# Retention scores of a fused two-block transformer: one f32 product per tile replaced by three products of rounded and remainder parts

## The chip, the cores and the metric

The kernel runs on one core of one Trainium2 chip. The metric is the device time of one launch in microseconds (us); where several runs are shown, the median is meant. The engines are TensorE (PE, with its weight loads listed as PEld), VectorE (DVE), ScalarE (ACT), GpSimd (POOL) and SyncE (SP), each with its own stream of instructions; they meet only in semaphores.

## The reference

Two blocks run one after the other on a sequence of 512 positions of width 1024; each has two layers. The change concerns the first block, whose layers begin with a projection of the normalised input and use its first 1024 columns as queries and keys of a retention with four heads of 128 channels:

```python
q = rotary(q.reshape(B, S, RET_HEADS, RET_QK_DIM), positions)
k = rotary(k.reshape(B, S, RET_HEADS, RET_QK_DIM), positions) * (RET_QK_DIM ** -0.5)
...
scores = jnp.einsum('bnihd,bnjhd->bnhij', qc, kc) * decay_intra.astype(dt)
intra = jnp.einsum('bnhij,bnjhe->bnihe', scores, vc)
...
o = rms_norm(o).reshape(B, S, RET_V_WIDTH)
return jax.nn.silu(g) * o
```

`rotary` multiplies the two halves of the 128 channels by cosines and sines of the position. The reference works in chunks of 128 with a carried state; the kernel computes the same sum directly over all causal pairs of positions, with the decay as a table. Everything is f32.

## The kernel before

**Layout and products.** All activations lie transposed, channels on the 128 partitions, positions along the free axis (S = 512). A wide product is made of three products of rounded operands: a value a is kept as aH (a rounded to the type fp32r) and aL = a - aH, and `three` (lines 575 to 579) sums wH·aH, wH·aL and wL·aH in PSUM. The weights come as a stream of 648 tiles of 128 x 1024, each good for 128 output columns (`tile_T`, 8 k-steps of three products, 24 in all) or, in `tiles_N`, for a quarter of 512 output columns whose results lie token by token.

**The ring.** Four slots hold the stream. SP loads tile n + 4 into `raw` when DVE has read tile n out of it (semaphore lo_ready, lines 401 to 404 and 427 to 432). ACT rounds it into `hi` (line 1316), as soon as it has landed and PE is done with the tile that used the slot (tile_done). DVE subtracts (line 1846: `lo` = raw - hi) and raises lo_ready, on which PE waits. Both engines do this in a function `tick` (ACT line 1306, DVE line 1835), which runs three tiles ahead of the tile at which it is called. Results go to PSUM banks 0 to 3 in turn; PE waits for bank_free before it uses a bank again.

**The stage of the change.** In each of the two layers the first eight tiles give the queries of heads 0 to 3 (n = 0 to 3) and the keys (n = 4 to 7). For tile n DVE runs `rotate(n)` (lines 2210 to 2221): two multiplications by cosine and sine tables and one on the other half of the channels, all from PSUM (lines 2215 to 2217, the last raises bank_free), a drain, an addition (line 2220) that leaves the rotated tile in A[:, n], a drain that raises rope_ready. The loop on DVE is `tick`, then `rotate` (lines 2223 to 2227); ACT only runs its ticks there (line 1527), and so has nothing to wait for but the slot. Tiles 0 to 2 of PE are computed together (`first_tiles`, `first_tiles_halved`), tile 3 alone, tiles 4 to 7 by `tiles_T`.

The next eight tiles are the values (`tiles_N(1)` twice, lines 642 to 658). Its first tile, tile 8 here, uses all four banks in turn, t = 0 to 3, with six products for each, and waits before each t for that bank, which `rotate(4 + t)` sets free.

**The scores.** `scores(h)` (lines 878 to 889) makes four products per head, one for each block j of 128 keys, of widths 512, 384, 256 and 128, from the f32 tiles A[:, 4 + h] and A[:, h]. DVE multiplies each by the decay (line 2233); the product j = 3 waits until DVE has read j = 0, because they share a bank. `scores(0)` comes after the first `tiles_N(1)`, `scores(1)` after the second, `scores(2)` and `scores(3)` between the products with the values (`weighted`, line 898) and the sums of squares (`square_sum`, line 908), which wait for ACT and POOL.

The order on each engine is written out by hand; there is no planner.

Of the kernel before, what the change touches and what calls it, by code (L numbers as in the profile page):

```python
# [7 lines left out]
F32 = mybir.dt.float32  # L8
F32R = mybir.dt.float32r
I32 = mybir.dt.int32  # L10
ACT = mybir.ActivationFunctionType
ALU = mybir.AluOpType
AX = mybir.AxisListType

P = 128
S = 512
# [4 lines left out]
R_HEADS, R_V = 4, 256  # L21
# [5 lines left out]
RING = 4  # L27
# [67 lines left out]
def build(nc, stream, first, xT, cvec, pos, consts, decay, tables, vec1, ws, bs, vec2, wf, outT):  # L95
    with ExitStack() as ctx:
# [3 lines left out]
        def sem(name):  # L100
            return ctx.enter_context(nc.semaphore(name))
# [19 lines left out]
        A, B, M = act3[:, 0:KT], act3[:, KT:2 * KT], act3[:, 2 * KT:3 * KT]  # L121
# [19 lines left out]
        pb = ctx.enter_context(nc.psum_tensor("pb", [P, 8, S], F32))  # L141
# [20 lines left out]
        rr_head = lambda h: yF[:, (6 + h % 2) * S:(7 + h % 2) * S]  # L162
        sqH = lambda h: yL[:, h % 2]
        sqL = lambda h: yL[:, 2 + h % 2]
        sumH, sumL, root_sq = halved[:, 4], halved[:, 5], act3[:, 7]
        meanF = meanR[:].bitcast(F32)
        root_y = yF[:, 14 * S:16 * S].rearrange("p (a s) -> p a s", a=2)
# [33 lines left out]
        score_bank = lambda h, j: (6, 7, 4 if h < 2 else 1, 6)[j]  # L201
# [76 lines left out]
        tile_done = sem("tile_done")  # L278
# [44 lines left out]
        x_added = sem("x_added")  # L323
        y_ready = sem("y_ready")
        rope_ready = sem("rope_ready")
        score_full = sem("score_full")
        score_ready = sem("score_ready")
        o_full = sem("o_full")
# [237 lines left out]
        def _(pe):  # L566
# [299 lines left out]
            for l in range(LAYERS):  # L866
# [10 lines left out]
                o_bank = lambda h: 2 + 2 * (h % 2)  # L877
                def scores(h):

                    pe.wait_ge(rope_ready, rope.value() + 5 + h)  # L880
                    for j in range(TT):
                        if j == 0 and h:

                            pe.wait_ge(score_ready, sc.value() + 4 * h)
                        if j == 3:

                            pe.wait_ge(score_ready, sc.value() + 4 * h + 1)
                        pe.matmul(pb[:, score_bank(h, j), 0:S - j * P], A[:, 4 + h, j * P:(j + 1) * P], A[:, h, j * P:S],
                                  start=True, stop=True).then_inc(score_full, 1)

                def weighted(h):

# [406 lines left out]
        def _(act):  # L1299
# [31 lines left out]
            def tiles_T(n, drain, uses_st=True, last=False, peel=False, ada=False, x_steps={}):  # L1331
                def body(i, first=False):
                    for s in range(RING):
                        t = None if not last else TILES - RING * (n // RING - i) + s
                        if ada:
                            for j in ADA_TICKS[s]:
                                tick(j, ada=j < RING)
                        elif s or not first:
                            tick(s, t)
                        act.wait_ge(tile_done, done.next())  # L1340
                        drain(i, s)
                if peel:
                    body(0, True)
                    bodies(n // RING - 1, {**({stf: RING} if uses_st else {}), **x_steps}, lambda i: body(i + 1))
                    return
                bodies(n // RING, {**({stf: RING} if uses_st else {}), **x_steps, **(dict(ada_ring) if ada else {})},
                       body, last)
# [166 lines left out]
            for l in range(LAYERS):  # L1514

                def drain_to(first, func):
                    def drain(i, s):
                        act.activation(act3[:, at(i * RING + s + first), :], pb[:, s:s + 1], func  # L1518
                                       ).then_inc(bank_free, 1)
                    return drain  # L1520

                def drain_tok(first, func):
                    def drain(i, t):
                        act.activation(act3[:, bass.ds(i + first + 2 * t, 1), :], pb[:, t:t + 1], func
                                       ).then_inc(bank_free, 1)
                    return drain
                tiles_T(8, lambda i, s: None, uses_st=False, peel=True)
                tiles_N(2, drain_tok(8, ACT.Copy))

                def head_out(h):  # L1530

                    for e in range(2):
                        o = pb[:, 2 + 2 * (h % 2) + e]
                        act.wait_ge(o_full, of.next())
                        act.activation(A[:, h + 4 * e], o, ACT.Copy)
                        act.activation(Osq[h % 2][:, e * S:(e + 1) * S], o, ACT.Square, scale=R_V ** -0.5
                                       ).then_inc(osq_ready, 1)

                def root_of(h):

                    act.wait_ge(summed, sums.next())
                    if h >= 2:
                        act.wait_ge(o_normed, 1 + 8 * l + 2 * (h - 1))
                    act.activation(r_head(h), pb[:, mean_bank(h)], ACT.Abs_reciprocal_sqrt, bias=epsc)
                    act.drain()
                    act.activation(rr_head(h), r_head(h), ACT.Square).then_inc(rooted, 1)

                def rounded_sum(h):

                    act.wait_ge(osq_added, oa.next())  # L1550
                    act.activation(sqH(h), Osq[h % 2][:, 0:S], ACT.Copy).then_inc(osq_rounded, 1)

                act.activation(cs[:, 2, 0:1], epsc, ACT.Abs_reciprocal_sqrt)
                head_out(0)
                rounded_sum(0)
                head_out(1)
                root_of(0)
                rounded_sum(1)
                head_out(2)
                root_of(1)  # L1560
                rounded_sum(2)
                head_out(3)
                root_of(2)
                rounded_sum(3)
                root_of(3)
                tiles_T(8, lambda i, s: to_st(s, func=ACT.Silu))
                pairs(True)
                tiles_N(2, drain_tok(8, ACT.Gelu_apprx_tanh), ada=True)
                act.wait_ge(v_mean, means.next())
                act.activation(stat[:, 8:12], stat[:, 12:16], ACT.Sqrt).then_inc(rooted, 1)  # L1570
                tiles_T(8, drain_to(0, ACT.Gelu_apprx_tanh), uses_st=False, ada=True)

                for n in range(KT):
                    s = n % RING
                    tick(s)
                    act.wait_ge(tile_done, done.next())
                    act.wait_ge(y_ready, l * 56 + (8 + n + 1))
                    act.activation(A[:, n], pb[:, s], ACT.Copy).then_inc(bank_free, 1)
                pairs()
                for g in range(4):  # L1580
                    tick(g)
                    act.wait_ge(tile_done, done.next())
                    for e in range(2):
                        n = 2 * g + e

                        to_st(n % 4, scale=v1[:, span(l * V_ALL + (V_PS + n), 1)], bias=bpps[:, n:n + 1])
                pairs(True)
                tick(0)
                to_x_halved(mod[:, 24:32], peel=True)
                tiles_T(8, lambda i, s: to_st(s), peel=True)  # L1590
                with repeat(act, 3, {split: 16, done: 16, stf: 8, **{c: 64 for c in land}}):
                    tiles_T(8, lambda i, s: None, uses_st=False)
                    tiles_T(8, lambda i, s: to_st(s))
                if l < LAYERS - 1:
                    to_x_halved(mod[:, 0:8])
                else:
                    act.wait_ge(gain_ready, 1)
                    late_tiles(to_late(hH, gain2, double=True))
# [213 lines left out]
        def _(dve):  # L1812
# [395 lines left out]
            for l in range(LAYERS):  # L2208

                def rotate(n):  # L2210

                    f = 1.0 if n < R_HEADS else float(P) ** -0.5
                    q = pb[:, n % RING]
                    dve.wait_ge(tile_done, done.next())
                    dve.scalar_tensor_tensor(A[:, n], q, f, cosT, ALU.mult, ALU.mult)
                    dve.scalar_tensor_tensor(rT[upper], q[lower], f, sinT[lower], ALU.mult, ALU.mult)
                    dve.scalar_tensor_tensor(rT[lower], q[upper], f, sinT[upper], ALU.mult, ALU.mult
                                             ).then_inc(bank_free, 1)
                    dve.drain()
                    dve.tensor_tensor(A[:, n], A[:, n], rT, ALU.add)  # L2220
                    dve.drain().then_inc(rope_ready, 1)

                for n in range(2 * R_HEADS):
                    if n:
                        tick(n % RING)
                    drained.next()
                    rotate(n)

                def decayed(h):
                    for j in range(TT):  # L2230
# [589 lines left out]
```

## Time and profile before

| | us |
|---|---|
| median of 3 runs | 3257.05 (3256.15 to 3257.8) |
| the profiled execution, its own time | 3255.68 |
| its span, first to last instruction | 3253.2 |
| PE busy | 3227.9 |
| DVE busy | 1900.5 |
| ACT busy | 1173.0 |
| POOL busy | 191.9 |

The span is the part of the execution that the trace covers; 2.5 us of the time lie around it. Busy time of PE counts from the start of a product to its modelled end, so neighbours overlap and gaps are hidden in it; the distance of two starts says more. In a timeline a row is start, duration, engine, line, operation, output <- input, count, and in brackets the idle time before it with the instruction that ended it.

### The profile page before, as it was taken

The page shows a single profiled execution, that of the slowest core. Times are in us where ns is not written, and L with a number is a line of the kernel's source. Part 1 is how long each engine was busy: PE and PEld are TensorE (multiplying, and loading weights), DVE is VectorE, ACT ScalarE, POOL GpSimd, SP SyncE. Part 2 cuts the span into 40 slices and gives each one's busy share as a digit, 9 for nine tenths or more (in the row PEclk, how much of TensorE's full clock was granted, in tenths as well). Part 3 has the DMA queues.
Part 4 walks back from the last instruction along what each step waited for, and adds up shares of the span by engine and source line. Part 5 has one row for each costly group of instructions (what it writes and reads, how often), then busy time and mean ns, then how long its engine had stood idle before and what let it go on. Part 6 is the DMA issues. An engine that isn't in the chain of part 4 may idle for free.

```text
span 3253.2 us, 43481 instructions
## 1 busy us (share of the span) xinstructions
PE 3227.9 (99%) x15288; PEld 2678.3 (82%) x15288; DVE 1900.5 (58%) x2749; ACT 1173.0 (36%) x1557; POOL 191.9 (6%) x202
## 2 busy tenths in 40 slices
PE   8999999999999999999999999999999999999998
PEld 7788888888888788888888888778888888988887
DVE  7454667564447454667564445656665744586656
ACT  4433333332223433343332233364333523453323
POOL 2100000100001100000100002021000101010001
PEclk9999999999999999999999999999999999999999
DMA  6146424422222145424422222202322322123222
GB/s 250 59 155 202 141 91 162 149 97 97 97 97 91 59 157 199 140 88 166 143 97 97 97 97 88 85 21 97 104 97 97 104 97 91 46 73 103 97 97 78
DMA packets 100057, 357.81 MB, mean 110 GB/s; under 512 B 11328, under 2 KB 13648, under 8 KB 99808
## 3 DMA queue, kind: packets, MB, share of 16 engines
q1 hardware_dynamic: 99248, 353.99, 32.5%
q0 software_dynamic: 688, 2.21, 0.2%
q8 instruction: 76, 1.25, 0.2%
q14 instruction: 45, 0.37, 0.0%
HBM read 354.06 MB, written 2.10 MB: 109 GB/s over the span
## 4 chain that ended last, share of the span: by engine, by line
PE 90%; issue 6%; DVE 1%; POOLq 1%; DMA 0%; ACT 0%; POOL 0%; DVEq 0%; ACTq 0%; SPq 0%
PE pb L577 24%; PE pb L579 24%; PE pb L578 24%; PE pb L607 2%; PE pb L608 2%; PE pb L611 2%; PE pb L1146 1%; PE pb L655 1%; PE pb L653 1%; PE pb L654 1%; PE pb L1247 1%; PE pb L1234 1%; PE pb L1249 1%; PE pb L1248 1%; PE pb L1080 1%
## 5 line engine op out<-in xcount | busy, mean ns | idle before, releaser
L1316 ACT ACTIVATE hi<-raw 128x1024 fp32r<-128x1024 f32 x549 | 577.4, 1056 | 1004.4 <-PE pb L579 685.8
L1846 DVE TENSOR_TENSOR lo<-raw,hi 128x1024 fp32r<-128x1024 f32 (+1 forms) x549 | 669.5, 1223 | 354.1 <-ACT hi L1316 307.3
L577 PE MATMUL pb<-yH,hi 128*128 128x512 f32 (+1 forms) x1664 | 644.2, 387 | 0.0
L579 PE MATMUL pb<-yH,lo 128*128 128x512 f32 (+1 forms) x1664 | 643.9, 387 | 0.0
L578 PE MATMUL pb<-yL,hi 128*128 128x512 f32 (+1 forms) x1664 | 643.9, 387 | 0.0
L577 PE MATMUL pb<-hH,hi 128*128 128x512 f32 x1528 | 596.4, 390 | 2.3 <-DVE lo L1846 2.2
L578 PE MATMUL pb<-hL,hi 128*128 128x512 f32 x1528 | 594.6, 389 | 0.0
L579 PE MATMUL pb<-hH,lo 128*128 128x512 f32 x1528 | 594.6, 389 | 0.0
L578 PEld LDWEIGHTS pb<-yL,hi 128*128 128x128 f32 x1664 | 312.4, 188 | 63.8
L579 PEld LDWEIGHTS pb<-yH,lo 128*128 128x128 f32 x1664 | 312.6, 188 | 63.6
L577 PEld LDWEIGHTS pb<-yH,hi 128*128 128x128 f32 x1664 | 312.5, 188 | 63.3
L577 PEld LDWEIGHTS pb<-hH,hi 128*128 128x128 f32 x1528 | 287.0, 188 | 62.5 <-ACT act L1518 3.0
L579 PEld LDWEIGHTS pb<-hH,lo 128*128 128x128 f32 x1528 | 286.8, 188 | 59.8
L578 PEld LDWEIGHTS pb<-hL,hi 128*128 128x128 f32 x1528 | 287.0, 188 | 58.6
L1329 ACT ACTIVATE st<-pb 128x512 f32<-128x512 f32 x176 | 105.4, 599 | 502.2 <-PE pb L579 496.3
L577 PE MATMUL pb<-halved,hi 128*128 128x512 f32 (+1 forms) x414 | 151.1, 365 | 0.5 <-DVE x L2648 0.3
L578 PE MATMUL pb<-halved,hi 128*128 128x512 f32 (+1 forms) x414 | 150.4, 363 | 0.0
L579 PE MATMUL pb<-halved,lo 128*128 128x512 f32 (+1 forms) x414 | 150.4, 363 | 0.0
L1825 DVE CUSTOM_DVE_ANT_0 raw<-raw,pb 128x1024 f32<-128x1024 f32 x96 | 112.6, 1217 | 39.5 <-ACT st L1329 24.2
L2051 DVE SCALAR_TENSOR_TENSOR x<-pb,mod,x 128x512 f32 x48 | 36.1, 752 | 137.5 <-PE pb L579 137.5
L2372 DVE SCALAR_TENSOR_TENSOR st<-st 128x512 f32<-128x512 f32 x64 | 44.3, 692 | 105.1 <-ACT st L1329 105.1
L2415 DVE TENSOR_TENSOR st<-pb,tab 128x512 f32<-128x512 f32 x88 | 60.8, 691 | 75.6 <-PE pb L579 66.2
(407 smaller groups left out, 3974.8 us busy)
## 6 DMA issues: line engine op xcount, KB each, us to landing
raw<-stream SPq DMA_DIRECT2D x648, 512.0 KB, 3.3
yF<-first SPq DMA_DIRECT2D x8, 512.0 KB, 13.3
act<-first SPq DMA_DIRECT2D x8, 512.0 KB, 16.1
x<-xT SPq DMA_DIRECT2D x4, 512.0 KB, 7.6
outT<-act SPq DMA_DIRECT2D x7, 256.0 KB, 2.2
tab<-decay SPq DMA_DIRECT2D x1, 1024.0 KB, 5.4
scr<-ws POOLq DMA_DIRECT2D x2, 256.0 KB, 3.0
scr<-bs POOLq DMA_DIRECT2D x2, 256.0 KB, 3.6
```

The costliest lines, as they stand in the source:

```text
L577: pe.matmul(out, whi, ahi, start=first, stop=False)
L578: pe.matmul(out, whi, alo, start=False, stop=False)
L579: return pe.matmul(out, wlo, ahi, start=False, stop=last)
L607: pe.matmul(pb[:, s], hi[:, s, w], aH[:, k], start=k == 0, stop=False)
L608: pe.matmul(pb[:, s], lo[:, s, w], aH[:, k], start=False, stop=False)
L611: ins = pe.matmul(pb[:, s], hi[:, s, w], aL[:, k], start=False, stop=k == ks - 1)
L1316: act.activation(hi[:, s], raw[:, s], ACT.Copy).then_inc(hi_ready, 1)
L1329: act.activation(st[:, s:s + 1], pb[:, b:b + 1], func, bias=bias, scale=scale).then_inc(bank_free, 1)
L1825: dve.tensor_tensor_reduce(w, w, c_all, 1.0, 0.0, ALU.mult, ALU.add, m).then_inc(lo_ready, 1)
L1846: dve.tensor_tensor(lo[:, s, 0:width], raw[:, s, 0:width], hi[:, s, 0:width].bitcast(F32), ALU.subtract).then_inc(lo_ready, 1)
L2372: dve.scalar_tensor_tensor(u, u, 0.0, u, ALU.max, ALU.mult)
L2415: dve.tensor_tensor(st[:, s], pb[:, s], rows, ALU.mult).then_inc(bank_free, 1)
```

## The change

The rotated tile is split like every other operand. ACT writes the rounded part of tile n after rope_ready says that DVE has rotated it; DVE writes the remainder, in its own order one tile later (after `rotate(n + 1)`). The rounded parts lie in free parts of yH and yL, the remainders in `halved`. The scores are then made by `three`, twelve products per head with fp32r operands in place of four with f32 operands, and PE waits for head_rest in place of rope_ready. ACT's stretch of eight bare ticks becomes a loop: tick, wait for the tile, wait for the rotation, round. As ACT works in order, its tick for the next slot now stands behind that wait.

```diff
+        head_hi = lambda n: yH[:, n % 4 + n // 4 * 2] if n % 4 < 2 else yL[:, 2 + n % 4 + n // 4 * 2]
...
+        head_rounded = sem("head_rounded")
+        head_rest = sem("head_rest")
...
                 def scores(h):
 
-                    pe.wait_ge(rope_ready, rope.value() + 5 + h)
+                    pe.wait_ge(head_rest, rope.value() + 5 + h)
                     for j in range(TT):
...
-                        pe.matmul(pb[:, score_bank(h, j), 0:S - j * P], A[:, 4 + h, j * P:(j + 1) * P], A[:, h, j * P:S],
-                                  start=True, stop=True).then_inc(score_full, 1)
+                        ks, qs_ = slice(j * P, (j + 1) * P), slice(j * P, S)
+                        three(pb[:, score_bank(h, j), 0:S - j * P], head_hi(4 + h)[:, ks], halved[:, 4 + h, ks],
+                              head_hi(h)[:, qs_], halved[:, h, qs_], True, True).then_inc(score_full, 1)
...
-                tiles_T(8, lambda i, s: None, uses_st=False, peel=True)
+                for n in range(2 * R_HEADS):
+                    if n:
+                        tick(n % RING)
+                    act.wait_ge(tile_done, done.next())
+                    act.wait_ge(rope_ready, 2 * R_HEADS * l + n + 1)
+                    act.activation(head_hi(n), A[:, n], ACT.Copy).then_inc(head_rounded, 1)
                 tiles_N(2, drain_tok(8, ACT.Copy))
...
+                def rest_of(n):
+
+                    dve.wait_ge(head_rounded, 2 * R_HEADS * l + n + 1)
+                    dve.tensor_tensor(halved[:, n], A[:, n], head_hi(n).bitcast(F32), ALU.subtract).then_inc(head_rest, 1)
+
                 for n in range(2 * R_HEADS):
                     if n:
                         tick(n % RING)
                     drained.next()
                     rotate(n)
+                    if n:
+                        rest_of(n - 1)
+                rest_of(2 * R_HEADS - 1)
```

## Rows read from the trace of the kernel before

**Rows 1.** The page, busy time by engine (share of the span) x instructions.

```profile
PE 3227.9 (99%) x15288; PEld 2678.3 (82%) x15288; DVE 1900.5 (58%) x2749; ACT 1173.0 (36%) x1557; POOL 191.9 (6%) x202
```

**Rows 2.** Waits of PE, whole span: us in total, times, longest.

```profile
PE pb L653 <- DVE act L2217: 2.0, 2, 1.5
```

**Rows 3.** Timeline of DVE, layer 0, rotation of tile 0 to that of tile 1.

```profile
50.57 0.69 DVE L2215 SCALAR_TENSOR_TENSOR act<-pb,tab 128x512 f32<-128x512 f32 x1
...
52.76 0.69 DVE L2220 TENSOR_TENSOR act<-act 128x512 f32<-128x512 f32 x1
53.57 1.22 DVE L1846 TENSOR_TENSOR lo<-raw,hi 128x1024 fp32r<-128x1024 f32 x1
54.82 0.69 DVE L2215 SCALAR_TENSOR_TENSOR act<-pb,tab 128x512 f32<-128x512 f32 x1
```

**Rows 4.** Timelines of PE and DVE, layer 0, tile 8 and the last rotation.

```profile
76.75 0.39 PE L653 MATMUL pb<-hi,hH 128*128 128x512 f32 x1
...
80.35 0.69 DVE L2215 SCALAR_TENSOR_TENSOR act<-pb,tab 128x512 f32<-128x512 f32 x1
...
80.60 0.39 PE L655 MATMUL pb<-lo,hH 128*128 128x512 f32 x1
82.50 0.50 PE L653 MATMUL pb<-hi,hH 128*128 128x512 f32 x1 [1.51 <-DVE act L2217]
```

**Rows 5.** The same in layer 1: first rotation, last rotation, PE behind it.

```profile
1023.75 0.69 DVE L2215 SCALAR_TENSOR_TENSOR act<-pb,tab 128x512 f32<-128x512 f32 x1 [2.44 <-PE pb L809]
...
1053.58 0.69 DVE L2215 SCALAR_TENSOR_TENSOR act<-pb,tab 128x512 f32<-128x512 f32 x1
...
1055.73 0.50 PE L653 MATMUL pb<-hi,hH 128*128 128x512 f32 x1 [0.48 <-DVE act L2217]
```

**Rows 6.** Timeline of ACT, layer 1, one tick of the eight.

```profile
1040.41 1.06 ACT L1316 ACTIVATE hi<-raw 128x1024 fp32r<-128x1024 f32 x1 [4.38 <-PE pb L579]
```

**Rows 7.** Timelines of DVE and ACT later on, where ACT follows a drained DVE result.

```profile
2215.17 0.68 DVE L1967 TENSOR_TENSOR x<-pb,x 128x512 f32<-128x512 f32 x1
...
2215.93 0.72 ACT L1420 ACTIVATE yH<-x,v 128x512 fp32r<-128x512 f32 x1 [0.43 <-DVEq L1971]
2216.56 0.62 ACT L1370 ACTIVATE act<-x 128x512 f32<-128x512 f32 x1
2217.08 1.05 ACT L1316 ACTIVATE hi<-raw 128x1024 fp32r<-128x1024 f32 x1
```

**Rows 8.** Line 1551, ACT rounding 128x512 from SBUF: duration ns min/median/max.

```profile
L1551 ACT ACTIVATE yL<-yF x8: 629/630/633, 133.7 to 1125.0; 128x512 fp32r<-128x512 f32 x8
```

**Rows 9.** Timeline of ACT and DVE, hand-over of a ring slot.

```profile
95.07 1.06 ACT L1316 ACTIVATE hi<-raw 128x1024 fp32r<-128x1024 f32 x1 [4.38 <-PE pb L655]
...
96.17 1.23 DVE L1846 TENSOR_TENSOR lo<-raw,hi 128x1024 fp32r<-128x1024 f32 x1 [4.21 <-ACT hi L1316]
```

**Rows 10.** Timelines of PE and DVE, scores of head 1 in layer 0.

```profile
124.33 2.32 PE L888 MATMUL pb<-act 128*128 128x512 f32 x8
...
125.39 1.73 DVE L2233 TENSOR_TENSOR act<-pb,tab 128x512 f32<-128x512 f32 x4 [3.98 <-PE pb L888]
126.48 4.48 PE L898 MATMUL pb<-act 128*128 128x512 f32 x16
```

**Rows 11.** Timeline of PE, 16 fp32r products 128 columns wide, then the next.

```profile
194.10 1.90 PE L638 MATMUL pb<-idR,csR 128*128 128x128 f32 x16
195.83 0.45 PE L577 MATMUL pb<-hH,hi 128*128 128x512 f32 x1
```

**Rows 12.** Windows of 1 us: busy us by engine, PEclk, DMA share, GB/s.

```profile
25.00:26.00 1.00, 0.36 (x2) 0.32 (x3) 0.99 (x1) 1.00 (x2) 0.82 (x2) 1.00 1.01 397
26.00:27.00 1.00, 1.00 (x6) 0.83 (x4) 0.35 (x2) 0.49 (x1) 0.99 (x1) 0.58 1.03 414
...
32.00:33.00 1.00, 1.00 (x3) 0.79 (x3) 1.00 (x3) 0.00 (x0) 0.97 (x1) 0.51 1.05 418
33.00:34.00 1.00, 1.00 (x6) 0.78 (x5) 1.00 (x1) 0.00 (x0) 0.82 (x2) 1.00 1.01 406
```

## The prediction

> **What bounds the kernel now.** I read four views, in this order. The busy times say that PE is the bound as a whole: 99% of the span, DVE 58%, ACT 36% [rows 1]. So fewer cycles on PE are worth their full time, and work on DVE and ACT costs nothing unless PE comes to wait for it. The waits of PE say where it already does: twice, once in each layer, its product at line 653 waits for line 2217, the last PSUM read of a rotation, 1.5 us at most and 2.0 us in total [rows 2]. The timeline shows which one. Tile 8 starts at 76.75, its first 18 products take 17 steps of 0.2265 us (to 80.60), and then t = 3 stands 1.51 us until the rotation of tile 7 has freed its bank [rows 4]; in layer 1 the same place waits 0.48 us [rows 5]. So the end of the eighth rotation is already on the path, with no slack. Last, the timeline of DVE: the loop of tick and rotation runs without a gap, 50.57 to 80.35 for seven passes in layer 0 and 1023.75 to 1053.58 in layer 1, 4.26 us a pass [rows 3 to 5]. ACT, before, idles 4.38 us ahead of a tick and waits for nothing but PE's slot [rows 6].
>
> **Part 1, the loop of rotations.** ACT now rounds tile n only after rope_ready, and its tick for the next slot stands behind that. DVE's next instruction but one is the subtraction that needs this tick, and its next rotation stands behind the subtraction. This closes a ring through both engines: rotation n, copy n on ACT, hi of tile n + 4 on ACT, lo of tile n + 4 on DVE, rotation n + 1. One pass, in order:
> - rotation, line 2215 to the end of line 2220: 52.76 + 0.69 - 50.57 = 2.88 us [rows 3];
> - drained DVE result to start on ACT: 2215.93 - (2215.17 + 0.68) = 0.08 us [rows 7];
> - the copy. The same form, 128x512 from SBUF to fp32r, takes 0.63 us [rows 8]; the next ACT instruction starts about 0.1 us before the end of its forerunner (a 0.62 us one is followed by hi after 0.52 us) [rows 7], so 0.53 us;
> - hi: 1.05 us [rows 7];
> - end of hi to lo: 96.17 - 96.13 = 0.04 us [rows 9];
> - lo to the next rotation: 54.82 - 53.57 = 1.25 us [rows 3].
>
> Sum 5.83 us, against 4.26 before: 1.57 us more per pass. The eighth rotation starts after seven passes, so 7 x 1.57 = 11.0 us later. PE waits for exactly this rotation already, so all of it is on the path: 11.0 us a layer, **22.0 us** in both. It does not add to what PE waits earlier, at lo of tiles 4 to 8, since those waits end before the last bank comes free; they only move PE back towards the same point. PE's own tile takes 24 x 0.2265 = 5.44 us, less than 5.83, so DVE never catches up. In tile 8, t = 2 and t = 3 wait for rotations one pass apart with 6 x 0.2265 = 1.36 us of work between: two gaps of about 4.5 us a layer.
>
> Bounds: the copy's share is between 0.53 and 0.72 us (line 1420, the costliest near relative [rows 7]), the two hand-overs have no row with two semaphore waits between, for which I allow 0.1 us more; if they overlap more than I think, 0.2 us less. That is 1.35 to 1.85 us a pass, 19 to 26 us in both layers. I take the middle, from the nearest rows.
>
> **Part 2, the remainder on DVE.** Eight subtractions of 128x512 a layer, 0.69 us like line 2220 [rows 3]. In the loop, that of tile n - 1 falls into DVE's wait of 0.08 + 0.53 + 1.05 + 0.04 = 1.70 us for hi: nothing. Without this cover it would add 0.69 us a pass, 9.7 us in all. Those of tiles 6 and 7 come after the last rotation, ahead of lo of tile 11. PE needs that one only two tiles after the end of tile 8, 10.9 us: nothing.
>
> **Part 3, other queues.** SP's load into a slot waits for lo and so moves with the passes, but it is asked for four passes, 23 us, before use: nothing. No step is added to POOL. PE's wait for head_rest of tile 4 + h comes a whole group of values after the loop: nothing.
>
> **Part 4, the scores.** Now 124.33 to 126.48, 2.15 us a head [rows 10]. At 2.4 GHz the 1280 columns at four cycles each are 2.13 us: f32 costs four passes. Three fp32r products at 0.2265 for 512 columns are 0.013 us above 512 cycles; with the same addition 384 and 256 columns cost 0.173 and 0.120 us. The narrow ones are 0.108 us each, 16 from 194.10 to 195.83 [rows 11]. Blocks 0 to 2 then take 3 x 0.520 = 1.56 us. Block 3 needs DVE's decay of block 0: it starts 1.06 us after PE now [rows 10], of which 0.85 are the four passes, so at 0.68 + 0.21 = 0.89, and ends 0.69 later at 1.58, 0.06 more to PE. Block 3 ends at 1.64 + 0.32 = 1.96 us: 0.19 us saved a head, **-1.5 us** for eight. Bounds: nothing, if the narrow products cost as much as f32; -4.4 us if only the columns counted (3 x 1280 at 2.4 GHz are 1.60 us, so 8 x 0.55).
> The Trainium skill (TensorE: Matmul & The Clock Gate, back-to-back issue gap) gives a sustained 81 ns for a 128-column product against the row's 108 ns, which would save another 0.6 us in all; the row is used.
>
> **Part 5, the clock.** The granted clock fell to half (1.2 GHz) in this very trace: 1.00 in 25 to 26 us, where PE was busy 0.36 us, 0.58 in the next, 0.51 in 32 to 33, and 1.00 again in 33 to 34 [rows 12]. Tile 8 will now offer PE some 10 us with one piece of 1.36 us in it, emptier than that. At half clock while it waits PE loses nothing; after the last bank is freed it loses half of what is left of the slow time. Between nothing and 3.5 us (half of those 7 us) a layer I take 1.7: **+3.4 us**.
> The Trainium skill (same page, part 1) says that the throttled state is the default and that activity releases it, and warns of PE idle gaps; by that rule the gaps would cost clock in both layers, which is the side I take.
>
> **Sum.** 22.0 - 1.5 + 3.4 = +23.9 us. The profiled execution took 3255.68, so 3279.6; the median is 1.4 above it, so 3281.0. I say 3280.
>
> **Rivals.**
> 1. *The ring, but the clock stays up*: +20.5, 3277. For it: shorter gaps of up to 1.5 us at the stop before cost no clock. Against: rows 12.
> 2. *Only DVE's own work counts*, ACT's copy and tick being ready in time: a pass is 4.26 + 0.73, the eighth rotation comes 5.1 us later, +10.2 - 1.5, about 3265. For it: ACT has 4 us idle a tick [rows 6]. Against: in program order the tick stands behind the wait.
> 3. *The other side: the three products decide.* Place: line 888; price: -1.5, at most -4.4 us; 3255. It decides only if a pass grows by less than 0.11 us (0.75 us saved per layer, over seven). For it: ACT is busy 36%. Against: the loop has neither a gap nor slack.
> 4. *The scores stay at four passes or gain nothing*: +25.4, 3282. It can hardly be told by time, but by the records.
>
> **How the numbers follow.** Forecast 0.55 (3280, itself 3275 to 3289), rival 1 0.28, rival 4 0.05, rival 2 0.07, rival 3 0.05. Range 3271 to 3289: from 19 - 4.4 with no clock loss (14.6, 3270.3) to 26 + 6.9 with no saving (32.9, 3288.6), rounded; it leaves out rivals 2 and 3, 0.12. Both ends of it are slower, so rivals 3 and a part of what I can't foresee are all that is not. A measurement of this kernel tells about 0.2% (6.5 us) from no change. Rival 3 lies within that except at its bound: faster by more 0.01, within 0.05, slower 0.94.
>
> **What would show it.** In the changed profile line 2215 starts every 5.8 us in both layers; lo waits for hi some 1 us in each pass; PE's line 653 has four waits near 4.5 us for line 2217's heir; the granted clock dips right behind them; the scores take about 1.95 us and have 96 records in place of 64. I am wrong if the distance of rotations stays near 4.3 or 5 us, if PE does not wait in tile 8, or if the time is under 3270.

## The result and the profile after

The changed kernel takes 3282.68 us (median of 4 runs, 3281.79 to 3283.85), the kernel before beside it 3256.86 us (3256.15 to 3257.8): 25.8 us more, a ratio of 1.0081 (95% interval 1.0068 to 1.0093). The forecast was 3280, in a range of 3271 to 3289.

| | before | after |
|---|---|---|
| profiled execution, its own time | 3255.68 us | 3283.85 us |
| span | 3253.2 us | 3281.9 us |
| mean granted clock of TensorE | 0.998 | 0.994 |
| PE busy | 3227.9 us | 3238.6 us |
| DVE busy | 1900.5 us | 1912.3 us |
| ACT busy | 1173.0 us | 1182.2 us |

The two profiled executions differ by 28.2 us in their own times, more than the medians do: the one after is the slowest of its four, and the one before was quicker than all four of its kernel here. DVE and ACT have 12 and 9 us more to do in 3282; neither is near full. PE stands idle for 43.3 us of the span in place of 25.3, and is busy 10.7 us longer, in part because some of its products run at half clock. In the waits of PE, whole span of the changed kernel (us in total, times, longest), line 2226 is what line 2217 was in [rows 2]:

```profile
PE pb L656 <- DVE act L2226: 16.1, 6, 4.2
...
PE pb L580 <- DVE lo L1855: 4.3, 4, 1.6
```

The cause is in the loop of rotations; a pass is the time from the start of one rotation to the start of the next. Timeline of DVE in the changed kernel, layer 0, one pass:

```profile
57.69 0.69 DVE L2224 SCALAR_TENSOR_TENSOR act<-pb,tab 128x512 f32<-128x512 f32 x1
...
59.87 0.69 DVE L2229 TENSOR_TENSOR act<-act 128x512 f32<-128x512 f32 x1
60.68 0.69 DVE L2235 TENSOR_TENSOR halved<-act,yH 128x512 fp32r<-128x512 f32 x1
62.30 1.23 DVE L1855 TENSOR_TENSOR lo<-raw,hi 128x1024 fp32r<-128x1024 f32 x1 [0.93 <-ACT hi L1320]
63.56 0.69 DVE L2224 SCALAR_TENSOR_TENSOR act<-pb,tab 128x512 f32<-128x512 f32 x1
```

And the timeline of ACT in the same pass:

```profile
60.69 0.63 ACT L1536 ACTIVATE yH<-act 128x512 fp32r<-128x512 f32 x1 [4.29 <-DVEq L2230]
61.23 1.04 ACT L1320 ACTIVATE hi<-raw 128x1024 fp32r<-128x1024 f32 x1
```

Both engines idle in every pass, each for the other: ACT 4.29 us for the drain behind the rotation, DVE 0.93 us for `hi` (1.74 in the first pass, which has no remainder in it yet). From 57.69 to 63.56 a pass is 5.87 us, where it was 4.26 [rows 3]. The remainder (line 2235, 60.68) lies wholly inside DVE's wait.

At the end of the loop stands tile 8. Timeline of PE in the changed kernel, layer 0, first products on the second, third and fourth bank, and the end of the slow stretch:

```profile
83.33 0.50 PE L656 MATMUL pb<-hi,hH 128*128 128x512 f32 x1 [0.47 <-DVE act L2226]
...
89.20 0.80 PE L656 MATMUL pb<-hi,hH 128*128 128x512 f32 x1 [4.21 <-DVE act L2226]
...
95.07 0.79 PE L656 MATMUL pb<-hi,hH 128*128 128x512 f32 x1 [2.94 <-DVE act L2226]
95.66 0.63 PE L657 MATMUL pb<-hi,hL 128*128 128x512 f32 x1
96.08 0.63 PE L658 MATMUL pb<-lo,hH 128*128 128x512 f32 x1
...
100.78 0.50 PE L657 MATMUL pb<-hi,hL 128*128 128x512 f32 x1
101.11 0.39 PE L658 MATMUL pb<-lo,hH 128*128 128x512 f32 x1
```

And in layer 1, third and fourth bank:

```profile
1076.23 0.50 PE L656 MATMUL pb<-hi,hH 128*128 128x512 f32 x1 [4.21 <-DVE act L2226]
...
1082.10 0.80 PE L656 MATMUL pb<-hi,hH 128*128 128x512 f32 x1 [3.75 <-DVE act L2226]
```

The products behind the fourth bank's wait take 0.43 us from start to start in place of 0.23, the mark of half clock. Windows of 2 us in the changed kernel (busy us of PE, PEld, DVE, ACT, POOL, then PEclk, DMA share, GB/s) show how it came about:

```profile
84.00:86.00 2.00, 0.99 (x5) 0.46 (x3) 0.96 (x3) 1.58 (x2) 0.00 (x0) 1.00 0.01 4
86.00:88.00 2.00, 0.00 (x0) 0.00 (x0) 1.96 (x3) 0.00 (x0) 0.00 (x0) 0.84 0.00 0
88.00:90.00 2.00, 0.80 (x2) 0.71 (x3) 1.82 (x3) 0.00 (x0) 0.00 (x0) 0.50 0.76 260
...
98.00:100.00 2.00, 2.00 (x6) 1.52 (x6) 1.64 (x2) 1.06 (x1) 0.00 (x0) 0.50 0.12 16
100.00:102.00 2.00, 2.00 (x8) 1.64 (x7) 0.34 (x1) 0.00 (x0) 0.00 (x0) 0.75 0.80 250
```

**The balance of the two profiled executions.** The first product of the scores of head 0, layer 0, before and after:

```profile
100.31 2.36 PE L888 MATMUL pb<-act 128*128 128x512 f32 x8
...
115.62 0.39 PE L580 MATMUL pb<-yH 128*128 128x512 f32 x1
```

Starts of the same instruction, before and after:
- the first rotation, 50.57 and 51.82: +1.25 us. It lies ahead of the change, in the start of the kernel, where PE waited 8.2 us in place of 6.8 for its first constants; it is no part of the change (experiment 2, with the same copies and remainders, has its first rotation at 50.32).
- first rotation to the product on the fourth bank in layer 0, 50.57 to 82.50 and 51.82 to 95.07: +11.32 us.
- from there to the first scores, to 100.31 and to 115.62: 17.81 and 20.55, +2.74 us, the clock. In layer 1 17.82 and 20.35, +2.53 us.
- from the first scores to the first projection tile after the heads, 49.76 and 49.44 in layer 0, 49.74 and 49.43 in layer 1: -0.6 us, the scores.
- from that tile of layer 0 to the product on the fourth bank in layer 1, 905.66 and 917.04: +11.38 us.

Together 1.25 + 22.70 + 5.27 - 0.6 = 28.6 us, and the spans differ by 28.7.

### The profile page after: what moved, and what is told of

Read it like the earlier page. It is cut to its first block, busy times and chain, and to the rows that moved or that the text cites. A ratio compares the mean times of both kernels' runs of the same rounds, so it can differ in the third digit from the quotient of the medians.

```text
span 3281.9 us, 43587 instructions
## 1 busy us (share of the span) xinstructions
PE 3238.6 (99%) x15320; PEld 2686.6 (82%) x15320; DVE 1912.3 (58%) x2765; ACT 1182.2 (36%) x1573; POOL 191.7 (6%) x202
## 3 DMA queue, kind: packets, MB, share of 16 engines
q8 instruction: 77, 1.26, 0.2%
## 4 chain that ended last, share of the span: by engine, by line
PE 89%; issue 7%; DVE 1%; POOLq 1%; DMA 0%; ACT 0%; POOL 0%; DVEq 0%; ACTq 0%; SPq 0%
PE pb L580 24%; PE pb L582 24%; PE pb L581 24%; PE pb L610 2%; PE pb L611 2%; PE pb L614 2%; PE pb L1150 1%; PE pb L657 1%; PE pb L658 1%; PE pb L656 1%; PE pb L1251 1%; PE pb L1238 1%; PE pb L1253 1%; PE pb L1252 1%; PE pb L1084 1%
## 5 line engine op out<-in xcount | busy, mean ns | idle before, releaser
L656 PE MATMUL pb<-hi,hH 128*128 128x512 f32 x256 | 103.6, 405 | 16.3 <-DVE act L2226 16.1
```

Of the source, the lines that this page charges most:

```text
L656: pe.matmul(pb[:, t], aH[:, k, a], hi[:, s, w], start=k == 0, stop=False)
```

## The experiments

All nine kernels compute the whole output. The kernel before was timed beside each group: 3255.74 us with experiments 1 to 4, 3256.80 with 5 to 7, 3255.99 with 8 and 9. These differ by 1 us, so between experiments of different groups, and with the changed kernel (3256.86 beside it), each time is compared by its distance to the kernel before beside it.

**1. ACT ticks before it waits.** The changed kernel, with ACT's order turned:

```diff
                 for n in range(2 * R_HEADS):
-                    if n:
-                        tick(n % RING)
                     act.wait_ge(tile_done, done.next())
+                    if n + 1 < 2 * R_HEADS:
+                        tick((n + 1) % RING)
                     act.wait_ge(rope_ready, 2 * R_HEADS * l + n + 1)
```

> Changed kernel, but ACT runs its tick for the slot that tile n has freed before it waits for rotation n; DVE's order is untouched. Ring theory (the tick behind the wait is the cost): the ring through ACT is open, a pass on DVE is its own work, 4.26 + 0.69 = 4.95 us, the eighth rotation comes 7 x 0.69 = 4.8 us a layer later than in the kernel before, PE's gaps in tile 8 shrink to about 2 to 3.6 us; with 0.7 us saved in the scores 3266 us, up to 3270 if the clock still falls. Rival (DVE's remainders and ACT's copies cost whatever their order): a pass stays at 5.87 us and the time at 3282.

Measured: 3266.45 us (3265.08 to 3266.87), ratio 1.0031 (1.0019 to 1.0043). Timeline of DVE in this kernel, layer 0, one pass:

```profile
64.95 0.69 DVE L2224 SCALAR_TENSOR_TENSOR act<-pb,tab 128x512 f32<-128x512 f32 x1
...
67.95 0.69 DVE L2235 TENSOR_TENSOR halved<-act,yL 128x512 fp32r<-128x512 f32 x1
68.56 1.22 DVE L1855 TENSOR_TENSOR lo<-raw,hi 128x1024 fp32r<-128x1024 f32 x1
69.81 0.69 DVE L2224 SCALAR_TENSOR_TENSOR act<-pb,tab 128x512 f32<-128x512 f32 x1
```

DVE waits no more and a pass is 4.86 us, its own work (4.26 in the first pass, which has no remainder). The tick in another place takes 15 of the 26 us away, with every copy and remainder still made. In the trace what is left is the remainder, 0.6 us in six passes a layer now that nothing hides it, 7.1 us in all; the clock, 1.60 us in layer 0 and 2.80 in layer 1 (0.50 in parts of both); and -0.6 us for the scores.

**2. DVE's remainders after the loop.** The changed kernel, ACT as it was:

```diff
                     rotate(n)
-                    if n:
-                        rest_of(n - 1)
-                rest_of(2 * R_HEADS - 1)
+                for n in range(2 * R_HEADS):
+                    rest_of(n)
```

> Changed kernel, ACT's order as it is, but DVE makes all eight remainders after the eighth rotation. Ring theory: they lay in DVE's wait for hi, so a pass stays at 5.87 us, DVE's idle time before lo grows from 0.92 to about 1.6 us, and the time stays at 3282 to 3283. Rival (the remainders are part of the cost): a pass loses up to 0.69 us, 9.7 us in all, 3273.

Measured: 3281.86 us (3280.86 to 3282.26), ratio 1.0078 (1.0063 to 1.0094). Timeline of DVE, layer 0:

```profile
67.93 0.69 DVE L2224 SCALAR_TENSOR_TENSOR act<-pb,tab 128x512 f32<-128x512 f32 x1
...
72.54 1.23 DVE L1855 TENSOR_TENSOR lo<-raw,hi 128x1024 fp32r<-128x1024 f32 x1 [1.74 <-ACT hi L1320]
73.80 0.69 DVE L2224 SCALAR_TENSOR_TENSOR act<-pb,tab 128x512 f32<-128x512 f32 x1
```

Without the remainder DVE waits 1.74 us in place of 0.93 and the pass stays at 5.87: in the changed kernel the remainders are free, as long as the ring through ACT is closed.

**3. Both moves.** The edits of 1 and 2 together.

> Changed kernel with both moves: ACT ticks before it waits for the rotation, DVE makes the remainders after the eighth rotation. Ring theory: a pass is back at 4.26 us, the eighth rotation where it was, the clock stays up, and only the scores' saving is left (0.7 us by the changed kernel's trace): 3256.2, within 0.5 us. Rival (splitting costs PE something that is not in this loop): 3258 or more.

Measured: 3255.34 us (3254.34 to 3255.69), ratio 0.9997 (0.9988 to 1.0006), a miss as it was put, 0.9 us under the expected 3256.2 where 0.5 was allowed. The expectation started from the kernel before at 3256.86; beside this run it stood at 3255.74, and the distance to it is -0.4 us where -0.7 was expected. The seven passes take 4.25 to 4.28 us in both layers. Waits of PE, whole span:

```profile
PE pb L656 <- DVE act L2226: 1.9, 2, 1.5
```

That is [rows 2] again, to 0.1 us. All work of the change is in this kernel, and no cost of it can be told from nothing: 26 us of the changed kernel (25.8 above the kernel before, against -0.4) hang on where two things stand in the order.

**4. The gaps filled.** The changed kernel, with 18 idle f32 products of 128 columns into a bank that nobody reads, ahead of PE's waits for the third and the fourth bank of tile 8:

```diff
                             if s == 0:
+                                if t >= 2:
+                                    for _ in range(busy):
+                                        pe.matmul(pb[:, 7, 0:P], ident, ones, start=True, stop=True)
                                 pe.wait_ge(bank_free, banks.next())
...
-                tiles_N(1, hH, hL)
+                tiles_N(1, hH, hL, busy=18)
```

> Changed kernel, but PE fills the gaps in tile 8: 18 f32 products of 128 columns (0.21 us each, 3.8 us) into an unused bank ahead of its waits for the third and fourth bank. They leave out nothing of the output. Clock theory: the granted clock stays at 1.00 in both layers, the last bank comes free at the same time, and the 2.7 us a layer lost at half clock return: 3277. Rival (the slow products behind the gap are not the clock, or the gaps are not its cause): 3282 to 3283.

Measured: 3278.49 us (3276.65 to 3278.84), ratio 1.0067 (1.0052 to 1.0083). The passes stay at 5.87 us. Windows of 8 us across both gaps of layer 0, columns as above:

```profile
84.00:92.00 8.00, 7.79 (x62) 7.30 (x61) 5.88 (x8) 2.70 (x4) 0.00 (x0) 1.00 0.19 66
92.00:100.00 8.00, 7.79 (x44) 6.65 (x44) 6.74 (x9) 2.54 (x3) 0.00 (x0) 1.00 0.28 87
```

The clock stays at 1.00 in both layers. The time is 3.4 us under that of experiment 2, which ran beside it with the same passes, and by the distances to the kernel before (22.8 and 25.8 us) 3.1 us under the changed kernel. It is 1.5 us above the expected 3277 and well under the rival's 3282. The idle gaps cause the slow stretch, and it is worth 3.1 to 3.4 us on the median. The two traces differ by more: 4.9 us from the first rotation to the end, since experiment 2 lost 5.3 us to the clock in its profiled execution.

**5. The wait alone.** The kernel before, with ACT's wait and nothing else of the change:

```diff
-                tiles_T(8, lambda i, s: None, uses_st=False, peel=True)
+                for n in range(2 * R_HEADS):
+                    if n:
+                        tick(n % RING)
+                    act.wait_ge(tile_done, done.next())
+                    act.wait_ge(rope_ready, 2 * R_HEADS * l + n + 1)
```

> Kernel before, with nothing of the change but ACT's wait: in its eight ticks ACT also waits for the rotation of the tile, and copies nothing. Ring theory: the pass is 2.88 + about 0.1 + 1.06 + 0.04 + 1.25 = 5.33 us, 1.07 more than before; the eighth rotation comes 7.5 us a layer later; two gaps of about 4 us a layer, so the clock may fall (up to 2.7 us a layer): 3272 without, 3277 with it. Rival (the cost is the work that was added, copies and remainders): 3257.

Measured: 3274.41 us (3273.60 to 3276.76), ratio 1.0054 (1.0039 to 1.0070). Timelines of ACT and DVE, layer 0:

```profile
70.13 1.06 ACT L1316 ACTIVATE hi<-raw 128x1024 fp32r<-128x1024 f32 x1 [4.29 <-DVEq L2225]
...
71.23 1.23 DVE L1850 TENSOR_TENSOR lo<-raw,hi 128x1024 fp32r<-128x1024 f32 x1 [1.20 <-ACT hi L1316]
```

A pass is 5.34 us. A wait that guards no work at all costs 17.6 us, two thirds of what the whole change costs: 14 passes longer by 1.08 us are 15.1, and the rest is the clock, which is at 0.50 in parts of both layers here too. The rival of added work (3257) is ruled out. The step from 5.34 to 5.87 is the copy, 0.53 us.

**6. f32 scores in the changed kernel.** Its loop as it is, the scores by one product a block, and the remainders in another place: `halved` shares its memory with `act3`, so that in the changed kernel a remainder overwrites the rotated tile.

```diff
-                        three(pb[:, score_bank(h, j), 0:S - j * P], head_hi(4 + h)[:, ks], halved[:, 4 + h, ks],
-                              head_hi(h)[:, qs_], halved[:, h, qs_], True, True).then_inc(score_full, 1)
+                        pe.matmul(pb[:, score_bank(h, j), 0:S - j * P], A[:, 4 + h, ks], A[:, h, qs_],
+                                  start=True, stop=True).then_inc(score_full, 1)
...
-                    dve.tensor_tensor(halved[:, n], A[:, n], head_hi(n)
+                    dve.tensor_tensor(yH[:, 4 + n] if n < 4 else yL[:, n - 4], A[:, n], head_hi(n)
```

> Changed kernel, but the scores are one f32 product each again, from the rotated tiles; copies, remainders and waits stay, the remainders go to unused tiles of yH and yL so that they don't overwrite the rotated ones. Ring theory: the loop is unchanged, 5.87 us a pass, and only the scores' own saving is given up: 0.7 us by the trace, 1.5 us by my forecast; 3283.4, at most 3284.5. Rival (more is gained or lost on PE by the split than the trace shows): outside 3281 to 3286.

Measured: 3281.43 us (3280.69 to 3282.21), ratio 1.0076 (1.0060 to 1.0091); a miss, 2 us under the expected 3283.4. The passes are at 5.87 us. In this execution the clock was back at 1.00 inside PE's second wait of layer 0, from about 91.5 us, and it was at 0.50 for a shorter time after: the stretch from the fourth bank to the first scores lost 1.60 and 2.20 us in the two layers, where the changed kernel's lost 2.74 and 2.53. What the clock takes varies from one traced execution to another by more than the scores are worth, so the median can't say what they are worth. The trace can, away from the clock: from the first scores to the first tile after the heads it takes 49.73 us in layer 0, the changed kernel 49.44.

**8. f32 scores, with both moves.** The edit of 6 on the kernel of 3, where no gap troubles the clock.

> The version with both moves, but with one f32 product for each score block again; the remainders go to unused tiles. It differs from the version with both moves in PE's products for the scores alone, with no gap and no clock in the way. By the changed kernel's trace a head's scores take 2.01 to 2.11 us against 2.12 to 2.16, about 0.7 to 0.8 us in all: 3256.0 where the version with both moves gave 3255.3. By my forecast 1.5 us: 3256.8. Rival (the split is worth nothing on PE): equal to the version with both moves.

Measured: 3255.99 us (3255.00 to 3256.79), ratio 1.0000 (0.9991 to 1.0009), 0.65 us above experiment 3, or 0.4 by the distances to the kernel before. The medians alone would not carry this; the traces do. From the first scores to the first tile after the heads layer 0 takes 49.43 us in experiment 3 (100.81 to 150.24) and 49.74 here (100.83 to 150.57), 0.31 us less for three rounded products. The changed kernel against the kernel before has 0.32 and 0.31 in the two layers, in the balance above. Timeline of PE in experiment 3, scores of head 0, from the last product of the third block:

```profile
102.26 0.29 PE L582 MATMUL pb<-yH,halved 128*128 128x256 f32 x1
102.50 0.33 PE L580 MATMUL pb<-yH 128*128 128x128 f32 x1
102.67 0.28 PE L581 MATMUL pb<-halved,yH 128*128 128x128 f32 x1
102.78 0.28 PE L582 MATMUL pb<-yH,halved 128*128 128x128 f32 x1
```

The narrow block starts 0.24 us after its forerunner, where 256 columns take 0.12: it waits for DVE's decay of block 0, whose bank it uses (DVE starts that at 101.76 and takes 0.69 us for 512 columns).

**7. The last rotation first.** The kernel of 3, and on DVE:

```diff
                 for n in range(2 * R_HEADS):
-                    if n:
+                    if 0 < n < 2 * R_HEADS - 1:
                         tick(n % RING)
                     drained.next()
                     rotate(n)
+                tick((2 * R_HEADS - 1) % RING)
```

> As the version with both moves, and DVE makes its last rotation before the tick that stood ahead of it, since PE waits for that rotation in tile 8 and for that tick's slot only two tiles later. The wait of 1.51 us in layer 0 and 0.48 us in layer 1 should shrink by 1.25 us (one lo) at most: 0.26 and 0 left, 1.7 us less than the version with both moves: 3254.5. Rival (PE then waits for the slot instead, or the time goes to a later wait): 3256.

Measured: 3252.76 us (3251.17 to 3253.87), ratio 0.9988 (0.9979 to 0.9997), the only kernel here whose interval lies below 1, by 4.0 us or 0.12%; 3254.5 was expected. Timeline of DVE, layer 0: the last two rotations stand 3.00 us apart, with no `lo` between.

```profile
76.64 0.69 DVE L2224 SCALAR_TENSOR_TENSOR act<-pb,tab 128x512 f32<-128x512 f32 x1
...
79.64 0.69 DVE L2224 SCALAR_TENSOR_TENSOR act<-pb,tab 128x512 f32<-128x512 f32 x1
...
82.64 1.23 DVE L1855 TENSOR_TENSOR lo<-raw,hi 128x1024 fp32r<-128x1024 f32 x1
```

PE's wait in tile 8 is 0.26 us in layer 0 and gone in layer 1.

**9. The same order in the kernel before.** The edit of 7 on the kernel before.

> Kernel before, nothing of the change, but DVE makes its last rotation ahead of the tick before it. If the gain over the kernel before of the version with both moves and this order comes from the order, this kernel has most of it: PE's waits in tile 8 shrink from 1.51 and 0.48 us to 0.26 and 0, 1.7 us off, 3255.1 with the kernel before at 3256.8. Rival (the gain came from the split): no change.

Measured: 3254.19 us (3252.94 to 3255.16), ratio 0.9994 (0.9985 to 1.0003), 1.8 us under the kernel before, as expected by the trace though within the interval. PE waits 0.22 us in layer 0. The order on DVE brings 1.7 to 1.8 us, the split 0.6. Their sum is 2.4, experiment 7 measured 4.0. The traces side with the sum: from the first rotation to the end the kernel before takes 3202.6 us, this one 3200.6 and experiment 7 3200.0, which is 2.6 less than the kernel before. The rest of the 4.0 is not in what these traces show of that stretch; whether it is more than scatter stays open.

## Why the prediction was right

**The bound, and where there was no slack.** The reading that the eighth rotation already sets the start of the fourth bank's products [rows 4, 5] carried the forecast. That the same delay would have cost less at a place with slack was not tried; here 11.32 and 11.38 us of 7 longer passes are on the path whole.

**The ring.** Forecast 5.83 us a pass, measured 5.87, and so 11.3 a layer in place of 11.0. Term by term in the trace after: rotation 2.87 (57.69 to 60.56), hand-over 0.13, copy 0.54, `hi` 1.04, hand-back 0.03, `lo` to the next rotation 1.26. Only the first hand-over was clearly too small, 0.13 where 0.08 us was taken from a place with one wait. Experiments 1, 3 and 5 show the mechanism from three sides: open the ring and the pass is 4.86, free DVE of the remainders too and it is 4.26, close it with nothing in it and it is 5.34.

**The remainder.** Forecast as free under the wait for `hi`, and at 0.69 us a pass without that cover. Experiment 2 shows the first and experiment 1 the second, at 0.60 (4.86 against 4.26), as neighbours on DVE overlap a little. This rules out rival 2 for the changed kernel; what it described, DVE's own work alone, is experiment 1, at 3266.45 where the rival had 3265. That the two agree so well is partly luck: the rival had 10.2 us of longer passes and no clock, experiment 1 had 7.1 and 4.4.

**The clock.** Forecast that it would fall in tile 8 and cost 1.7 us a layer; in the profiled execution it was 2.74 and 2.53. The step was right in kind, and in the profiled execution this term, the middle between two bounds, was too small by 1.9 us over the two layers. The slow stretch that counts ran from the fourth bank to about 5.8 us later in layer 0 (95.07 to 100.9). The forecast had four waits near 4.5 us; they were 4.21, 2.94, 4.21 and 3.75, since the third bank's products, at half clock, took up a part of the last wait. The same stretch, from the fourth bank's first product to the first scores, in the profiled executions (us; the loss is against 17.8 a layer):

| | layer 0 | layer 1 | loss |
|---|---|---|---|
| kernel before | 17.81 | 17.82 | |
| changed kernel | 20.55 | 20.35 | 5.3 |
| 1, tick first | 19.41 | 20.62 | 4.4 |
| 2, remainders after | 20.55 | 20.37 | 5.3 |
| 4, gaps filled | 17.82 | 17.81 | 0 |
| 5, wait alone | 20.71 | 20.39 | 5.5 |
| 6, f32 scores | 19.41 | 20.02 | 3.8 |

Experiment 4 puts the whole term at 3.1 to 3.4 us on the medians, and what the ring and the scores leave of the 25.8 is 3.7, both near the 3.4 forecast. That an ordinary execution loses less than the profiled ones follows from the medians alone; no trace shows it. Rival 1 (clock stays up) is ruled out by the windows above.
The Trainium skill (TensorE: Matmul & The Clock Gate, part 1) has the throttled state follow from want of activity; by that rule, which the forecast followed, the traces agree: 1.00 with the gaps filled, 0.50 with them empty.

**The scores.** This is the step that was off: -1.5 us was forecast, -0.6 measured, in experiments 3 and 8 and in the balance above. A head takes 2.01 to 2.11 us in place of the 1.96 worked out. The fp32r products of 512, 384 and 256 columns are as forecast (0.227, 0.17, 0.12 us). Three things were missed: in head 0 the narrow block starts at 1.70 us, 0.06 later than worked out; its first product takes 0.16 us, not 0.108, since it starts behind a wait; and in head 2 the first fp32r product behind f32 ones takes 0.31 us (145.87 to 146.18), not 0.227. The Trainium skill's 81 ns for a narrow product (TensorE: Matmul & The Clock Gate, back-to-back issue gap) would have moved the sum further off: after the first, they start 0.11 us apart in the changed kernel (117.48 and 117.59). Rival 4, no saving, misses by 0.6 us, and rival 3, in which these products decide, is what experiment 3 shows once the order is mended: 0.4 us faster than the kernel before, well within what can be told from no change.

**The sum.** Forecast +23.9 us, median +25.8: ring +22.7 in place of 22.0, clock 3.7 by what is left of the median (5.3 in the trace) in place of 3.4, scores -0.6 in place of -1.5. All three errors point the same way, so none hid another. The rest of the distance from 3280 to 3282.68 is that 3281.0 was put as 3280. Two slips in the range change nothing here: its ends were added to 3255.68 and the forecast to a median 1.4 higher, and two layers of 3.5 us went in as 6.9.

## What to carry to other kernels

On an in-order engine a new wait holds up everything that is queued behind it, and the question to ask is whether the engine that is waited for needs any of that: if it does, the two run in lockstep, at the sum of their steps, however idle both are. Put the work that others need first and the new, patient work behind it; here two moves took back all of 26 us. And look for the place where the bound engine already waits for the changed loop: a delay there is paid in full, and a small reordering there pays too: the last rotation ahead of a subtraction whose slot is needed only two tiles later brought 1.8 us to the kernel before, though within its interval.

## What the runs showed of the hardware

TensorE's granted clock also fell behind a shorter wait than the two of about 4.5 us that were forecast. In experiment 1 PE waited 1.63 and 3.19 us in layer 0 with 1.4 us of work between, and the clock was at 0.50 in the window from 87.6 to 89.6 us; in layer 1 it waited 0.60 and 3.18, and the clock fell as well. In the kernel before, a single wait of 1.51 us at this place left it at 1.00. The slow stretch was also longer than the wait ahead of it: in the changed kernel's two layers, behind waits of 2.94 and 3.75 us, PE ran dense products at half clock for 5.8 and 5.3 us before it was back at 1.00. And it is not the same in two executions with the same waits: experiment 6, with the passes of the changed kernel, had the clock back at 1.00 inside the second wait of layer 0, the changed kernel had not.
